# A fused two-model layer stack in emulated fp32: new work orders in its attention stages and feed-forward starts

## The chip, the cores and the metric

One NeuronCore of a Trainium2 chip runs the whole program, one launch, batch 1, 256 tokens, width 1024. The metric is device time in microseconds (us); smaller is better.

## The reference, cut to what matters

Two transformer models follow each other. The first has two layers: layer 0 mixes tokens with a gated delta rule beside an mLSTM, layer 1 with windowed attention (16 query heads in 4 groups, sinks). After each mixer come a squared-ReLU feed-forward and a gated addition. The second model has two layers with five attentions side by side (low-rank, forget-gated, block, differential, and one over a memory of 256 tokens) and a gated feed-forward with a short convolution. What the change touches:

```python
h = h + rmsnorm(ff, gains[3])                       # "post" factor, first model
gate = jax.nn.sigmoid(h @ w_ple_gate[layer])
h = h + gate * (p[layer] @ w_ple[layer])
...
q_e = _rms_norm(_heads(mem_q, N_HEADS_GROUP), mem_q_norm[l])
mem_kv = _rms_norm(mem, mem_norm[l]) @ mem_w_kv[l]
k_e, v_e = [_heads(t, N_HEADS_GROUP) for t in jnp.split(mem_kv, 2, axis=-1)]
o_e = _memory_attention(q_e, _rms_norm(k_e, mem_k_norm[l]), v_e, HEAD_DIM ** -0.5)
...
x = x + mixed @ w_o[l]
```

## The kernel before, in words

**Products.** Every large product is made of three fp32r matmuls (high by high, high by low, low by high; L495 to L497). Weights land in three raw slots by DMA from SyncE's queue. ScalarE casts a half of a panel to its high part (`scalar_split`, L684), VectorE subtracts to get the low part (`vector_split`, L786). There are four slots for such halves, so a cast waits until TensorE has used the half four before, and `split(upto)` runs up to three parts past `upto`. Activations are split in the same way (`hT`, `aT`, `memT`).

**Order.** There is no planner. Each engine has its own program, written out by hand, and semaphores tie them; an engine never overtakes a waiting instruction. The eight PSUM banks are filled in turn (`Banks.fill`): TensorE waits until the bank whose turn it is was read; banks that are still held for a long sum are passed over.

**Attention** (`tensor_attention`, `scalar_attention`, `vector_attention`). Groups of four heads go through a skewed pipeline. In step i TensorE does, in this order: the transposes of the output of group i-4 (`out_turned`), values of group i-3, transposes of the probabilities of i-2 (`turned`), scores of i-1, output products of i-4 (a panel of 48 matmuls into four held banks), and the transposes of queries and keys of group i (`prepared`). VectorE moves scores out of PSUM (L2180 to L2184), finds row maxima (L2190), and scales values (L2244). ScalarE does the exponentials (L2107), copies queries and keys (L2087/L2089), copies probabilities (L2124). Between these, generators (`between`, `amid`, `work`) put in other work: in the first model's layer 1 (mixer c, groups 0 to 3) the projection of the memory for both later layers (`mem_kv`, eight parts of 12 matmuls), in the second model's mixers (mixer 2, groups 0 to 5) the last columns of `w_in`. Group 5 of mixer 2 is the attention over the memory.

**Mixer 2, names.** Its queries are divided by their root mean square: squares on ScalarE, sums on VectorE, `means`, a square root on ScalarE (L716), a reciprocal on VectorE (L805), and a product (L2634). Outputs of finished groups are split into `m.out`, which is one slot of two chunks of `hT` here (`slots` = 1), four slots in mixer c.

**Starts of feed-forwards.** The sum of squares over features is taken by matmuls with ones: L667 over pairs 0 to 2, L670 over the last pair's squares, which ScalarE makes in `scalar_last_squares` (L741). After a feed-forward of the first model, L653/L658 do the same by token, then a root, a reciprocal, and L518 spreads the factor. `vector_turn_tables` builds the angles for sines and cosines, ScalarE applies Sin (L1720).

## Time and profile before

| | |
|---|---|
| median of 3 runs | 1517.23 us (1515.94 to 1520.54) |
| profiled execution, its own time | 1518.34 us |
| its span | 1517.0 us |
| mean granted TensorE clock | 0.979 |
| PE / DVE / ACT / POOL busy | 96% / 66% / 51% / 7% |
| moved by DMA | 228.19 MB, mean 150 GB/s |

PE is TensorE's matmul side, DVE VectorE, ACT ScalarE, POOL GpSimd. Positions in the text are us from the start of the span. A busy PE includes matmuls at half clock, so the granted clock has to be read beside it.

### The profile page before, as it was taken

What the parts mean: (1) busy time and instruction counts of PE and PEld (TensorE: products, weight loads), DVE (VectorE), ACT (ScalarE), POOL (GpSimd) and SP (SyncE); (2) the same over time, 40 slices, a digit from 0 to 9 for tenths busy, and PEclk for the clock granted to TensorE, in tenths of its full rate; (3) what the DMA queues carried; (4) which work ended last, traced back from release to release, by engine and by line L of the source; (5) the groups of instructions that cost most, each with busy time, mean ns of one, the idle gap of its engine ahead of it and who ended that gap; (6) DMA issues with size and microseconds to landing.
All of it is one profiled execution on the core that took longest, in us unless ns stands there. A gap on an engine that the chain in (4) does not pass through costs nothing.

```text
span 1517.0 us, 26059 instructions
## 1 busy us (share of the span) xinstructions
PE 1451.9 (96%) x10884; PEld 1376.7 (91%) x10884; DVE 997.7 (66%) x1503; ACT 777.5 (51%) x1219; POOL 110.4 (7%) x100
## 2 busy tenths in 40 slices
PE   7999989999998889999999989999999998999999
PEld 7989979999986789999997779999998787899999
DVE  5575676654678657654486765877755676577763
ACT  6744445444474544444376665544445685543443
POOL 0014112100001001110000000011100000011100
PEclk9999989999999999999999988999999998999999
DMA  8532245555463236655544312556555421255553
GB/s 260 161 111 84 61 155 179 191 182 182 158 202 132 73 107 190 184 182 194 180 155 153 120 59 72 176 170 190 175 193 189 137 84 56 90 181 177 190 177 105
DMA packets 186573, 228.19 MB, mean 150 GB/s; under 512 B 5964, under 2 KB 161228, under 8 KB 186456
## 3 DMA queue, kind: packets, MB, share of 16 engines
q1 hardware_dynamic: 185448, 221.75, 45.7%
q0 software_dynamic: 1008, 4.77, 0.9%
q8 instruction: 86, 1.41, 0.4%
q14 instruction: 31, 0.25, 0.1%
HBM read 225.46 MB, written 1.05 MB: 149 GB/s over the span
## 4 chain that ended last, share of the span: by engine, by line
PE 70%; DVE 17%; ACT 8%; issue 3%; DMA 1%; POOL 0%; DVEq 0%; ACTq 0%; SPq 0%; POOLq 0%
PE bank L495 20%; PE bank L497 20%; PE bank L496 20%; DVE weights_low L786 6%; ACT weights_high L684 3%; PE bank L503 2%; PE bank L1002 2%; ACT S L2107 2%; PE bank L2052 2%; DVE cv L2910 1%; PE bank L2031 1%; DVE S L2182 1%; DVE cv L2907 1%; DVE pad L2897 1%; DMA weights_raw<-in_w_in_ab 1%
## 5 line engine op out<-in xcount | busy, mean ns | idle before, releaser
L786 DVE TENSOR_TENSOR weights_low<-weights_raw,weights_high 128x1024 fp32r<-128x1024 f32 (+2 forms) x421 | 507.2, 1226 | 289.4 <-ACT weights_high L684 289.2
L684 ACT CAST weights_high<-weights_raw 128x1024 fp32r<-128x1024 f32 (+2 forms) x421 | 424.7, 1031 | 257.1 <-PE bank L497 254.8
L495 PE MATMUL bank<-hT_high,weights_high 128*128 128x256 f32 x1640 | 472.1, 288 | 15.3 <-DVE hT_low L858 5.0
L496 PE MATMUL bank<-hT_low,weights_high 128*128 128x256 f32 x1640 | 467.6, 285 | 0.0
L497 PE MATMUL bank<-hT_high,weights_low 128*128 128x256 f32 x1640 | 467.6, 285 | 0.0
L495 PEld LDWEIGHTS bank<-hT_high,weights_high 128*128 128x128 f32 x1640 | 318.1, 194 | 20.9 <-issue 9.8
L496 PEld LDWEIGHTS bank<-hT_low,weights_high 128*128 128x128 f32 x1640 | 318.0, 194 | 0.3
L497 PEld LDWEIGHTS bank<-hT_high,weights_low 128*128 128x128 f32 x1640 | 317.7, 194 | 0.2
L495 PE MATMUL bank<-aT_high,weights_high 128*128 128x256 f32 x864 | 242.3, 280 | 0.2
L496 PE MATMUL bank<-aT_low,weights_high 128*128 128x256 f32 x864 | 241.2, 279 | 0.0
L497 PE MATMUL bank<-aT_high,weights_low 128*128 128x256 f32 x864 | 241.1, 279 | 0.0
L495 PEld LDWEIGHTS bank<-aT_high,weights_high 128*128 128x128 f32 x864 | 162.2, 188 | 0.6 <-DVE weights_low L786 0.6
L497 PEld LDWEIGHTS bank<-aT_high,weights_low 128*128 128x128 f32 x864 | 162.3, 188 | 0.0
L496 PEld LDWEIGHTS bank<-aT_low,weights_high 128*128 128x128 f32 x864 | 161.7, 187 | 0.0
L495 PE MATMUL bank<-weights_high,hT_high 128*128 128x512 f32 (+1 forms) x288 | 115.0, 399 | 6.7 <-DVE weights_low L786 5.3
L497 PE MATMUL bank<-weights_high,hT_low 128*128 128x512 f32 (+1 forms) x288 | 111.2, 386 | 0.0
L496 PE MATMUL bank<-weights_low,hT_high 128*128 128x512 f32 (+1 forms) x288 | 111.2, 386 | 0.0
L2107 ACT ACTIVATE S<-S,mx 128x256 f32<-128x256 f32 (+1 forms) x128 | 57.2, 448 | 71.9 <-DVE mx L2190 49.7
L495 PEld LDWEIGHTS bank<-weights_high,hT_high 128*128 128x128 f32 x288 | 54.8, 190 | 19.5 <-DVE weights_low L786 6.1
L497 PEld LDWEIGHTS bank<-weights_high,hT_low 128*128 128x128 f32 x288 | 54.9, 191 | 10.4
L2862 ACT ACTIVATE cv<-cv 128x512 f32<-128x512 f32 x22 | 13.9, 633 | 95.9 <-DVE cv L2910 95.9
L496 PEld LDWEIGHTS bank<-weights_low,hT_high 128*128 128x128 f32 x288 | 55.0, 191 | 8.8
(417 smaller groups left out, 1830.8 us busy)
## 6 DMA issues: line engine op xcount, KB each, us to landing
weights_raw<-in_w_up SPq DMA_DIRECT2D x32, 1024.0 KB, 5.4
weights_raw<-in_w_down SPq DMA_DIRECT2D x32, 1024.0 KB, 5.1
weights_raw<-in_ffn_w_gate SPq DMA_DIRECT2D x22, 1024.0 KB, 5.3
weights_raw<-in_ffn_w_up SPq DMA_DIRECT2D x22, 1024.0 KB, 5.3
weights_raw<-in_w_in SPq DMA_DIRECT2D x20, 1024.0 KB, 5.0
weights_raw<-in_w_in_ab SPq DMA_DIRECT2D x16, 1024.0 KB, 5.9
weights_raw<-in_ffn_w_down SPq DMA_DIRECT2D x16, 1024.0 KB, 5.5
weights_raw<-in_w_o SPq DMA_DIRECT2D x10, 1024.0 KB, 6.1
```

The lines of the kernel that those rows point to most:

```text
L495: k.E.matmul(out, xh, wh, start=first, stop=False)
L496: k.E.matmul(out, xh, wl, start=False, stop=False)
L497: return k.E.matmul(out, xl, wh, start=False, stop=last)
L503: mm = k.E.transpose(bank[0:src.shape[-1], i * P:(i + 1) * P], src, k.ident)
L684: k.A.copy(w.halves(n)[0], w.raw_part(n)).then_inc(*k.s.weight_high(n))
L786: k.V.tensor_tensor(low, w.raw_part(n), high.bitcast(F32), ALU.subtract).then_inc(*k.s.weight_low(n))
L1002: mm = k.E.matmul(bank[:, hd * P:(hd + 1) * P], x(hd), y(hd), start=True, stop=True)
L2031: mm = E.matmul(bank[:, x * nk:(x + 1) * nk], m.QK[i][p0:p0 + d, c, t * P:(t + 1) * P], m.QK[i][p0:p0 + d, g.key_block(c), 0:nk], start=Tr ...
L2052: mm = E.matmul(bank[:, (t * 4 + hh) * 64:(t * 4 + hh + 1) * 64], m.PT[:, b, hh, :], g.values(hh, u), start=(x == 0), stop=(x == len(block ...
L2107: e = A.activation(m.S[:, i, hh, c0:c0 + nk], m.S[:, i, hh, c0:c0 + nk], ACT.Exp, bias=m.mx[:, i, t, hh:hh + 1], accum_out=m.den[:, i, t, ...
L2182: op = V.scalar_tensor_tensor(dst, bank, g.scale, spread(g.mask[:, c0:c0 + nk], 1, per), ALU.mult, ALU.add)
L2897: V.tensor_tensor(m.pad[:, q, :, 2:], k.banks[key][:, :].rearrange("p (k n) -> p k n", k=2), R, ALU.mult).then_inc(*k.banks.read(key))
```

## The change

Feed-forwards (both models): ScalarE makes the last pair's squares ahead of its first casts. The sine and cosine tables of layer 0 are built during the down projection. The sums by token after a feed-forward of the first model go into the next panel of 16 products: four products, the sums, three products, then the factor's transposes.

Mixer c: products are read out of their banks ahead of the last split of their panel; the keys are rotated before the memory is split; ScalarE alone copies queries and keys; two memory parts run at the first call instead of one; casts for the memory weights follow the steps 0, 0, 3, 3, 5, 5, 7; the memory's banks are read in `work(2)` and `work(4)` (ends of steps 1 and 3), and the second half of the query heads is rotated in `work(2)` instead of `work(1)`.

Mixer 2: two casts go ahead of the exponentials of group 0; one low half is made while a root is under way. The memory queries are no longer multiplied by their inverse root: their scores are, as they leave PSUM (sum plus 64 eps, so that the scale 1/8 is contained). The root for that is in `finish(3)` (step 6), no longer in `work(5)` (step 4). `m.out` has two slots.

All three attentions: the output of the last group is transposed amid the products of the group before it, after 9 of its 16.

```diff
@@ -811,14 +811,18 @@
     vector_inverse(k, st, r)
 
 
-def vector_token_linear(k, key, n0, evacuate=None, between=None):
+def vector_token_linear(k, key, n0, evacuate=None, between=None, evacuated_first=False):
     for k0 in (0, 4):
         n = k.w.first(key + (k0, n0))
         for i in range(2):
-            vector_split(k, n + i + 1)
-            if k0 + 2 * i == DC - 2 and evacuate is not None:
+            last = k0 + 2 * i == DC - 2 and evacuate is not None
+            if not (last and evacuated_first):
+                vector_split(k, n + i + 1)
+            if last:
                 for t in range(NT):
                     evacuate(t)
+            if last and evacuated_first:
+                vector_split(k, n + i + 1)
             if between is not None:
                 next(between, None)
 
...
@@ -1709,20 +1713,16 @@
     tensor_feature_major(k, ("p", layer), m.pt, 2)
     for p in range(4):
         tensor_pair_panels(k, st, p, m.aT, DFF1 // P, ("down", layer), lambda c: s.active.at((st, c - c % 2)))
-    tensor_sums_by_token(k, (st, "post"))
 
 
 def scalar_feed_forward_1(k, layer):
     A, s, m, st = k.A, k.s, k.ff1[layer], ("ff1", layer)
-    if layer == 0:
-        for which in range(2):
-            A.wait_ge(*s.angles.at(which))
-            A.activation(k.trig_table[:, which, :, :], k.trig_table[:, which, :, :], ACT.Sin).then_inc(*s.trig(which))
     for n0 in range(0, DFF1, 256):
         c, i = n0 // P, n0 // 256 % 2
+        if c == 0:
+            scalar_last_squares(k, st)
         scalar_split(k, k.w.first(("up", layer, 0, n0)) + 2)
         if c == 0:
-            scalar_last_squares(k, st)
             scalar_sums_root(k, st, m.R)
         A.wait_ge(*k.banks.was_read((st, c)))
         A.activation(m.aT[0][:, c:c + 2, :].rearrange("p k n -> p (k n)"), m.r[:, i, :], ACT.Square).then_inc(*s.relu_high((st, c)))
@@ -1731,6 +1731,10 @@
         for k0 in range(0, DFF1 // P, 8):
             scalar_split(k, k.w.first(("down", layer, k0, 256 * p)) + 2)
         scalar_out_squares(k, st, p)
+        if layer == 0 and p == 1:
+            for which in range(2):
+                A.wait_ge(*s.angles.at(which))
+                A.activation(k.trig_table[:, which, :, :], k.trig_table[:, which, :, :], ACT.Sin).then_inc(*s.trig(which))
     scalar_sums_root(k, (st, "post"), m.post_inv)
     for p in range(4):
...
@@ -1769,8 +1773,6 @@
 
 def vector_feed_forward_1(k, layer):
     V, s, m, st = k.V, k.s, k.ff1[layer], ("ff1", layer)
...
@@ -1793,6 +1795,8 @@
         for k0 in range(0, DFF1 // P, 8):
             vector_split(k, k.w.first(("down", layer, k0, 256 * p)) + 2)
         vector_out_gained(k, st, p, m.u, post_gain(k, layer, 1))
+        if layer == 0 and p == 0:
+            vector_turn_tables(k)
     vector_add_post(k, st, m, ("gate", layer), k.ple[layer].hT, None)
 
 
...
@@ -1820,8 +1824,11 @@
     held = tensor_hold(k, pst)
 
     def post_factor():
-        yield
-        yield
+        for _ in range(3):
+            yield
+        tensor_sums_by_token(k, (("ff1", layer), "post"))
+        for _ in range(3):
+            yield
         tensor_along_tokens(k, (("ff1", layer), "post"), k.ff1[layer].post_inv)
     tensor_deep_panel(k, pst, held, k.ff1[layer].pT, 0, ("ple", layer, 0, 0), k.banks.was_read((pst, "T", 0)), True, True, post_factor())
...
@@ -1919,33 +1926,41 @@
     vector_rms(k, "mem", m.inv)
 
 
+
+MEMORY_SPLITS = (0, 0, 3, 3, 5, 5, 7)
+
+
 def tensor_memory_projected(k):
 
-    for l in range(2):
-        yield from tensor_token_parts(k, ("mem", l), ("mem_kv", l), k.mem.memT[l], 0, 512)
+    parts = itertools.chain(*[tensor_token_parts(k, ("mem", l), ("mem_kv", l), k.mem.memT[l], 0, 512) for l in range(2)])
+    next(parts)
+    for _ in parts:
+        yield
 
 
 def scalar_memory_projected(k):
 
     n = k.w.first(("mem_kv", 0, 0, 0))
-    for part in range(8):
-        scalar_split(k, n + part - part % 2)
+    for upto in MEMORY_SPLITS:
+        scalar_split(k, n + upto)
         yield
 
 
 def vector_memory_projected(k):
 
-    n, m = k.w.first(("mem_kv", 0, 0, 0)), k.mem
-    for part in range(8):
-        vector_split(k, n + part - part % 2)
-        if part % 4 == 3:
-            l = part // 4
-            k.V.wait_ge(*k.s.inverse.at("mem"))
-            for t in range(NT):
-                key = (("mem", l), 0, t)
-                k.V.wait_ge(*k.s.products.at(key))
-                k.V.tensor_scalar(k.kvm[l][:, t, :], k.banks[key][:, :], m.inv[:, t:t + 1], None, ALU.mult).then_inc(*k.banks.read(key))
-        yield
+    n = k.w.first(("mem_kv", 0, 0, 0))
+    for upto in MEMORY_SPLITS:
+        vector_split(k, n + upto)
+        yield
+
+
+def vector_memory_evacuated(k, l):
+
+    k.V.wait_ge(*k.s.inverse.at("mem"))
+    for t in range(NT):
+        key = (("mem", l), 0, t)
+        k.V.wait_ge(*k.s.products.at(key))
+        k.V.tensor_scalar(k.kvm[l][:, t, :], k.banks[key][:, :], k.mem.inv[:, t:t + 1], None, ALU.mult).then_inc(*k.banks.read(key))
 
 
 def in_pairs(hh):
...
@@ -2054,6 +2075,10 @@
         mm.then_inc(*s.products((st, "values", n)))
 
     def out_turned(n):
+        if n < len(a.groups) - 1:
+            out_turned_now(n)
+
+    def out_turned_now(n):
         if a.groups[n].out is not None:
             E.wait_ge(*a.finished(k, n))
             tensor_feature_major(k, (st, "out T", n), a.groups[n].out[0], 2)
@@ -2066,7 +2091,14 @@
             held.extend(tensor_hold(k, st))
         _, j, k0 = g.out
         ready = k.banks.was_read(((st, "out T", n), "T", 0))
-        tensor_deep_panel(k, st, held, a.out, 2 * (j % a.slots), a.key + (k0, 0), ready, j == 0, n == len(a.groups) - 1)
+        amid = last_turned() if n == len(a.groups) - 2 else iter(())
+        tensor_deep_panel(k, st, held, a.out, a.out_chunk(n), a.key + (k0, 0), ready, j == 0, n == len(a.groups) - 1, amid)
+
+    def last_turned():
+
+        for _ in range(DC):
+            yield
+        out_turned_now(len(a.groups) - 1)
 
...
@@ -2079,7 +2111,7 @@
     before = a.slot_before(n)
     if before is not None:
         k.A.wait_ge(*k.s.products.at(a.last_scores(before)))
-    for c in range(0, g.blocks, 2 if a.copies_by_scalar else 4):
+    for c in range(0, g.blocks, 2):
         key, w = (st, "qk", n, c), min(2, g.blocks - c)
...
@@ -2180,6 +2198,8 @@
                     op = V.scalar_tensor_tensor(dst, bank, g.scale, g.bias[:, own, c0:c0 + nk], ALU.mult, ALU.subtract)
                 elif g.mask is not None:
                     op = V.scalar_tensor_tensor(dst, bank, g.scale, spread(g.mask[:, c0:c0 + nk], 1, per), ALU.mult, ALU.add)
+                elif g.query_factor is not None:
+                    op = V.tensor_tensor(dst, bank, spread(g.query_factor[:, t, own], 2, nk), ALU.mult)
                 else:
                     op = V.tensor_scalar(dst, bank, g.scale, None, ALU.mult)
...
@@ -2336,16 +2357,18 @@
             x = m.proj[:, t, c0:c0 + n * CHD].rearrange("p (n d) -> p n d", d=CHD)
             vector_rope(k, x, n, ROT_C, 0, t, m.tmp1, m.tmp2, ("c", c0, t))
     projected(1024)
+    turned_heads(1024, 4, 1024)
     vector_memory_turned(k)
     projected(0)
-    turned_heads(1024, 4, 1024)
     turned_heads(0, 8, 0)
     projected(512)
     V.tensor_scalar(m.minus_sink, k.row(1, "sinks"), -1.0, None, ALU.mult).then_inc(*s.minus_sink("c"))
     V.wait_ge(*s.minus_sink.at("c"))
 
     def work(n):
-        if n == 1:
+        if n in (2, 4):
+            vector_memory_evacuated(k, n // 2 - 1)
+        if n == 2:
             turned_heads(512, 8, 512)
 
...
@@ -2405,9 +2428,10 @@
         Group(4, P, in_fours(0), 32 ** -0.5, True, values(C_DIFF + 512), None, mask=cneg, gains=heads_2(k, l, "diff")),
         Group(4, P, in_fours(1), 32 ** -0.5, True, values(C_DIFF + 512), out(2), mask=cneg, shared=True),
         Group(4, P, in_pairs, 64 ** -0.5, True, values(C_MOBA + 512), out(3), mask=cneg, gains=heads_2(k, l, "moba")),
-        Group(4, P, in_pairs, 64 ** -0.5, False, lambda hh, u: kvm[:, u, 256 + hh * 64:256 + (hh + 1) * 64], out(4), gains=heads_2(k, l, "mem")),
+        Group(4, P, in_pairs, 64 ** -0.5, False, lambda hh, u: kvm[:, u, 256 + hh * 64:256 + (hh + 1) * 64], out(4), gains=heads_2(k, l, "mem"),
+              query_factor=m.st[:, :, SLOT["memq"]:SLOT["memq"] + 4]),
     ]
-    return Attention(("m2", l), m, groups, 1, ("o_2", l), m.out, copies_by_scalar=True, late=(1,))
+    return Attention(("m2", l), m, groups, 2, ("o_2", l), m.out, copies_by_scalar=True, late=(1,))
 
 
 def projected_to(k, l, end):
...
@@ -2485,7 +2509,6 @@
             for mark in projected_to(k, l, D_IN2):
                 E.wait_ge(*mark)
         else:
-            E.wait_ge(*s.normed.at((l, "memq")))
             for mark in projected_to(k, l, D_IN2):
                 E.wait_ge(*mark)
...
@@ -2563,8 +2586,8 @@
         n2, n5 = [k.w.first(("in_2", l, 0, n0)) for n0 in (2048, 2560)]
         squared_columns("moba", C_MOBA, 512)
         scalar_root(k, (st, "mla"), m.st2[:, :, 0:20])
-        yield
-        scalar_split(k, n2 + 1)
+        scalar_split(k, n2 + 2)
+        yield
         for t in range(NT):
             evacuated(2048, t)
         squared_columns("diff", C_DIFF, 512)
@@ -2583,14 +2606,11 @@
             scalar_split(k, k.w.first(("in_2", l, 0, 2560)) + 4)
             squared_columns("memq", C_MEM, 256)
 
-    def work(n):
-        if n == 5:
-            roots("memq", SLOT["memq"], 4)
-
     def finish(n):
         if n == 3:
+            roots("memq", SLOT["memq"], 4)
             scalar_root(k, (st, "sub"), m.st2[:, :, 0:4])
-    scalar_attention(k, k.attention_2[l], work, finish, last_columns(), amid)
+    scalar_attention(k, k.attention_2[l], None, finish, last_columns(), amid)
     for p in range(4):
         scalar_residual(k, ("ff2", l), p, st, k.hT, ff2_gain(k, l))
 
...
@@ -2648,9 +2671,13 @@
         V.wait_ge(*s.products.at((st, n0, t)))
         V.tensor_scalar(m.hp[:, t, n0:n0 + nn], k.banks[st, n0, t][:, 0:nn], m.inv[:, t:t + 1], None, ALU.mult).then_inc(*k.banks.read((st, n0, t)))
 
-    def scaled(*kinds):
+    def scaled(*kinds, meanwhile=lambda: None):
         first, end = SLOT[kinds[0][3]], SLOT[kinds[-1][3]] + kinds[-1][1]
-        inverses(kinds[0][3], m.st[:, :, first:end], spread(k.const("inv_d")[:, first:end], 1, NT))
+        name, x = kinds[0][3], m.st[:, :, first:end]
+        means(name, x, spread(k.const("inv_d")[:, first:end], 1, NT))
+        meanwhile()
+        vector_inverse(k, (st, name), x)
+        V.wait_ge(*s.inverse.at((st, name)))
         for c0, n, d, name in kinds:
             normed(name, m.hp[:, :, c0:c0 + n * d], n, m.st[:, :, SLOT[name]:SLOT[name] + n],
...
@@ -2722,7 +2749,7 @@
         vector_split(k, n2 + 1)
         yield
         squared(DIFF)
-        scaled(DIFF)
+        scaled(DIFF, meanwhile=lambda: vector_split(k, n2 + 2))
         turned_heads("diff", C_DIFF, 16, 32, ROT_D, ROT_C + ROT_A + ROT_M)
...
@@ -2777,10 +2804,13 @@
             vector_split(k, k.w.first(("in_2", l, 0, 2560)) + 4)
 
     def work(n):
+
         if n == 5:
             squared(MEMQ)
-            scaled(MEMQ)
+            V.wait_ge(*s.reduced.last())
+            V.tensor_scalar(queries, queries, 64 * EPS, None, ALU.add).then_inc(*s.mean((st, "memq")))
     a = k.attention_2[l]
...
@@ -2798,7 +2828,10 @@
             then(V.scalar_tensor_tensor(m.d1, m.d2, m.lm[:, 66:67], m.d1, ALU.mult, ALU.add))
             then(V.tensor_tensor(m.d2, m.d1, m.d1, ALU.mult))
             V.tensor_reduce(m.st2[:, :, 0:4], m.d2.rearrange("p t (n d) -> p t n d", n=4), AXX, ALU.add).then_inc(*s.reduced((l, "sub")))
-            inverses("sub", m.st2[:, :, 0:4], 1.0 / 64)
+            means("sub", m.st2[:, :, 0:4], 1.0 / 64)
+            vector_inverse(k, (st, "memq"), queries)
+            vector_inverse(k, (st, "sub"), m.st2[:, :, 0:4])
+            V.wait_ge(*s.inverse.at((st, "sub")))
             for t in range(NT):
...
@@ -2854,9 +2887,10 @@
     A, s, m, st = k.A, k.s, k.ff2[l], ("ff2", l)
     for n0 in range(0, DFF2, 256):
         c, i = n0 // P, n0 // 256 % 3
+        if c == 0:
+            scalar_last_squares(k, st)
         scalar_split(k, k.w.first(("ff_gate", l, 0, n0)) + 2)
         if c == 0:
-            scalar_last_squares(k, st)
             scalar_sums_root(k, st, m.R)
         A.wait_ge(*s.conv.at((st, c, 1)))
         A.activation(m.cv[:, i, :, :], m.cv[:, i, :, :], ACT.Silu).then_inc(*s.silu((st, c)))
```

## Rows read from the trace of the kernel before

**Rows 1.** The page: the span.
```profile
span 1517.0 us, 26059 instructions
```
**Rows 2.** Waits of PE over the span: what waited for what, total us, times, longest.
```profile
PE bank L495 <- DVE weights_low L786: 7.6, 4, 2.7
...
PE bank L670 <- ACT pair_squares L741: 4.9, 3, 3.2
...
PE bank L495 <- DVE hT_low L796: 4.3, 3, 1.5
```
**Rows 3.** Windows: stretch, length, busy (x) PE PEld DVE ACT POOL, PEclk, DMA, GB/s.
```profile
224.31:228.60 4.29, 4.29 (x21) 4.20 (x20) 2.44 (x2) 1.14 (x3) 0.62 (x1) 0.50 0.79 244
...
893.29:949.34 56.05, 49.74 (x355) 46.04 (x353) 29.72 (x49) 33.12 (x79) 0.00 (x0) 0.85 0.23 75
1256.39:1312.48 56.09, 47.88 (x354) 43.95 (x353) 29.73 (x49) 32.82 (x79) 0.00 (x0) 0.88 0.22 74
...
587.00:754.00 167.00, 166.63 (x1404) 166.66 (x1404) 93.79 (x95) 72.00 (x79) 19.30 (x17) 1.00 0.59 189
```
**Rows 4.** Timeline, feed-forward start of layer 0: start, length, engine, line, [idle before <-releaser].
```profile
218.55 0.38 PE L667 MATMUL bank<-pair_sum,consts 128*128 128x256 f32 x1
...
222.80 0.80 PE L670 MATMUL bank<-pair_squares,consts 128*128 128x256 f32 x1 [3.22 <-ACT pair_squares L741]
...
224.31 0.78 PE L495 MATMUL bank<-hT_high,weights_high 128*128 128x256 f32 x1
```
**Rows 5.** Timeline of PE, feed-forward start of layer 1.
```profile
579.33 0.38 PE L667 MATMUL bank<-pair_sum,consts 128*128 128x256 f32 x1
...
587.37 0.35 PE L495 MATMUL bank<-hT_high,weights_high 128*128 128x256 f32 x1 [0.41 <-DVE weights_low L786]
```
**Rows 6.** Timeline of PE, behind the feed-forward of layer 0.
```profile
399.76 0.38 PE L658 MATMUL bank<-consts,pair_squares 128*128 128x1 f32 x2 [0.90 <-ACT pair_squares L741]
...
401.82 0.27 PE L518 MATMUL bank<-consts,post_inv 128*128 128x128 f32 x1
...
410.24 0.35 PE L495 MATMUL bank<-gate_hT_high,weights_high 128*128 128x256 f32 x1 [0.41 <-DVE gate_hT_low L856]
```
**Rows 7.** Timeline of PE in the first mixer 2.
```profile
865.39 0.43 PE L495 MATMUL bank<-weights_high,hT_high 128*128 128x356 f32 x1 [2.68 <-DVE weights_low L786]
...
898.80 0.30 PE L503 MATMUL bank<-consts,S 128*128 128x128 f32 x1 [1.42 <-ACT QK L2089]
...
902.37 0.47 PE L503 MATMUL bank<-consts,S 128*128 128x128 f32 x1 [2.43 <-DVE hT_low L796]
```
**Rows 8.** Timeline of ACT in the first mixer 2.
```profile
899.25 1.28 ACT L716 ACT_TABLE_LOAD   x1
900.54 0.21 ACT L716 ACTIVATE st<-st 128x8 f32<-128x8 f32 x1
900.66 0.57 ACT L695 CAST hT_high<-bank 128x512 fp32r<-128x512 f32 x1
...
925.11 0.51 ACT L2107 ACTIVATE S<-S,mx 128x256 f32<-128x256 f32 x1 [4.31 <-DVE mx L2190]
```
**Rows 9.** Timeline of DVE in the first mixer 2.
```profile
901.63 0.68 DVE L796 TENSOR_TENSOR hT_low<-bank,hT_high 128x512 fp32r<-128x512 f32 x1
...
907.66 0.69 DVE L2182 SCALAR_TENSOR_TENSOR S<-bank,consts 128x512 f32<-128x512 f32 x1 [0.15 <-PE bank L2031]
...
921.46 2.48 DVE L2184 TENSOR_SCALAR S<-bank 128x512 f32<-128x512 f32 x4 [0.20 <-DVE mixed L2806]
```
**Rows 10.** Timeline of DVE in mixer c.
```profile
474.94 0.41 DVE L946 TENSOR_TENSOR tmp<-proj,trig 128x256 f32<-128x256 f32 x1
...
479.19 1.28 DVE L2182 SCALAR_TENSOR_TENSOR S<-bank,consts 128x512 f32<-128x512 f32 x2
...
494.06 1.41 DVE L1947 TENSOR_SCALAR kvm<-bank,mem_inv 128x512 f32<-128x512 f32 x2
```
**Rows 11.** Timeline of PE in mixer c.
```profile
494.87 0.48 PE L503 MATMUL bank<-consts,k 128*128 128x128 f32 x1 [2.04 <-DVE kvm L1947]
```

39 lines of the change are left out of this document (16 added, 23 removed).

## The prediction

> **What bounds the kernel now.** I read the page first, then the waits of TensorE (PE), then windows for its clock, then the timeline around each idle stretch. The profiled execution took 1518.34 us, its span is 1517.0 us [rows 1], so 1.34 us lie around the span. The median of the runs shown is 1517.23, 1.1 below the profiled one. PE is busy for 96% of the span, so a gain is idle PE time or half-clock time that comes back. Two kinds of stretch must be told apart. In the first model's second up-and-down projection 1404 matmuls take 167 us at clock 1.00, 0.119 us each, with no idle time [rows 3]: there PE is the bound, and a microsecond won at the start stays won. In the attention stages matmuls are short, and the work goes round PE, VectorE (DVE) and ScalarE (ACT).
>
> The second kind is seen in the two mixers 2. From the query transposes of group 4 to the last output panel the first takes 56.05 us at a mean clock of 0.85, the second 56.09 us at 0.88 [rows 3]. The engine that had the better clock gained nothing. So a chain through DVE and ACT bounds most of this stretch, and PE's idle time there is the result of it.
>
> **Feed-forward starts.** In layer 0, PE has summed three pairs at 218.55 and waits 3.22 us for the last squares, since ACT first does two sine tables and two casts; L670 starts at 222.80, the next features at 224.31 [rows 4]. The wait is followed by a stretch at 0.50, in which 21 matmuls take 4.29 us [rows 3]. A panel has 48; the other 27 take 27 x 0.119 = 3.2. So from L667 to the next panel: 5.76 + 4.29 + 3.2 = 13.25 us. The change takes both causes away, and layer 1, which has no tables there, is the pattern: 587.37 - 579.33 = 8.04, with a wait of 0.41 for a low half included [rows 5]. Gain **5.2**. Bounds: 3.2, the wait alone; 6.0, if the 0.41 goes too.
>
> In the two gated feed-forwards the squares wait behind casts only. PE's waits for L741 are 4.9 us in three, the longest 3.2 [rows 2], so the two others have 1.7. ACT now waits for a pair sum ahead of its casts, but PE still has four ready halves. Gain **1.7** (bounds 0 and 1.7; in layer 1 of the first model there is no such wait, so nothing).
>
> The tables move into the down projection. DVE needs some 3 us for them, while a half there lasts 24 x 0.119 = 2.9 us of PE and four are ready, so they are hidden; if that cover is gone, they cost up to 3. ACT must load the square root's table again, 1.28 us [rows 8], beside PE's products.
>
> **Sums amid products (two places).** Now L658 starts at 399.76 after a wait of 0.90, and L518 at 401.82, 2.06 later with three products between [rows 6]. In the new order PE does four products (12 matmuls, 1.4 us) ahead of the sums and nothing waits: L653 starts at 397.9 + 1.4 = 399.3, L658 0.9 later at 400.2, L518 at about 402.25. The idle 0.90 is filled, but the factor comes 0.4 us later, and what ends last behind it is DVE's chain to the next activations: PE waits for them at 410.24 anyway [rows 6]. So this edit *costs* 0.4 each, **-0.9** together (bounds: -1.5, and +0.9 each if that second wait were not there).
>
> **Last output turned amid products (three places).** PE's waits in L495 for L796 are 4.3 us in three, longest 1.5 [rows 2]. These are the waits in front of the last output panel. The transposes now come after 9 of 16 products, some 2.5 us before that panel begins, and need ACT 0.57 and DVE 0.68 [rows 8, 9]. All 4.3 go, 1.43 per stage. The second slot of `m.out` makes that possible and takes no wait away by itself.
>
> **Mixer 2 (two of them, alike).** First, PE's 2.68 us for a low half at 865.39 [rows 7] go, as cast and low half are made ahead. But the casts stand in front of the exponentials of group 0: the second waits for PE's second part, and the exp table (1.28) is loaded behind it, so these start nearly 1 us later. And behind the wait the next thing that ends late is group 1's exponentials and the copies behind them. Of 2.68 I take half, 1.3 (bounds 0 and 2.7).
>
> Second, in step 4 ACT does table load and root for the memory queries (899.25 to 900.66) before it copies group 1's output [rows 8]: 1.4 off the queue. DVE then has no product L2634 in front of its low part (901.63 [rows 9]), 0.4 more. So PE's third transposed block moves from 902.37 [rows 7] by 1.3 + 1.4 + 0.4 = 3.1. Its wait of 2.43 becomes some 0.6.
>
> Third, the clock. From 902.37 to the last scores that DVE takes at 907.66 [rows 9] are 5.3 us for 4 transposes and 16 score matmuls, at half clock; at full clock it would be 2.9. If the clock holds, the scores are 3.1 + 2.4 = 5.5 earlier, and with them the exponentials of group 4, the casts, the copies of group 5 and DVE's work on the differential output. The root now sits there beside one that already needed the square root's table, so it adds no load; it adds one reciprocal (0.2). Scores of group 5 leave PSUM by a product of two operands instead of one with a constant: L2182, with two tensors, has 0.68 to 0.69 for 512 elements, L2184 2.48 for four [rows 9], so nothing. Exponentials of group 5 (925.11 [rows 8]) start 5.3 earlier, and PE, whose panel of 48 needs 5.8 us, is not late for them.
>
> With the last panel: 5.3 + 1.4 = 6.7. If the clock does not hold: 4.3; with a second half-clock stretch under the late panel: 2.8. Which? New idle time of 1.4 and 0.6 us stands close together in short matmuls; before it was 1.42 and 2.43. That lies between what lost the clock and what did not, so I take **5.4** for each mixer, last panel included.
>
> The Trainium skill (TensorE: Matmul & The Clock Gate, Terms) prices time at half clock at half of it. By that rule the mixers at 0.85 and 0.88 would lose 8.4 and 6.7 us to the clock, and the second should be 1.7 us shorter; rows 3 have them equal, so the trace disagrees for this stage. In the dense stretch of layer 0 it agrees (21 matmuls, 4.29 instead of 2.5 us). It gives the first rival below its most.
>
> The skill (ScalarE: Activation LUTs, What ACT_TABLE_LOAD costs) counts 1.28 us and a drain of 1.38 for each change of table set. In rows 8 the root starts 0.01 us after the load: no drain. By the rule the exponentials of group 0 would start 1.4 us later still, and the sum would be up to 2.8 us smaller.
>
> **Mixer c.** DVE before: rotation of the second query heads from 474.94, the first scores taken only at 479.19 [rows 10]. With the rotation moved, and one memory part more before the scores, I count scores 3.4 us earlier and one part (2.75 us) ahead. But then the memory's banks: their reads wait for `work(2)`, behind three low halves. By the order of `Banks.fill` the transposed probabilities of group 0 now fall on those two banks (before, they were passed over as held), and the values of group 1 on the next two. I put these waits at 4.3 and 4.7 us; before one such wait took 2.04 [rows 11], and a pair of reads takes 1.41 [rows 10]. The rotation (4.25 us) now stands in front of the scores of group 1. By step 4 the lead is used up: first output panel at 525 to 527, before at 524. So -0.5 there and +1.4 for the last panel: **+0.9** (bounds: -12 and +6).
>
> **Sum.** 5.2 + 1.7 - 0.9 + 2 x 5.4 + 0.9 = 17.7. On the profiled execution 1518.34 - 17.7 = 1500.6; 1.1 lower for the median: **1499.5 us**.
>
> **Rivals.**
> A. The clock holds and mixer c keeps its lead. Mixers 2 give 6.7 each, mixer c 4.3 + 1.4: 5.2 + 1.7 - 0.9 + 13.4 + 5.7 = 25.1, so 1492. For: each wait has its cause named. Against: the bank order. The rule on half-clock time would add all of mixer 2's low-clock time, another 15 us: 1477. I give that 3 in 100.
> B. The wait moves. In both mixers the clock stays low and the panel is slowed (2.8 each), mixer c loses 6: 5.2 + 1.7 - 0.9 + 5.6 - 4.6 = 7.0, 1510.
> C. Slower: the memory's banks in mixer c. If none of their delay overlaps: bank waits 4.3 + 4.7, rotation 4.0, low halves in front of group 2's scores 1.9, half-clock stretches behind both waits 3.4 each, together 21.7, and mixers 2 as in B: 5.2 + 1.7 - 0.9 + 5.6 + 1.4 - 21.7 = -8.7, 1526. It decides from about 13 us of loss in mixer c. Against: the DVE delays lie inside the bank waits.
> D. No change: mixers 2 give nothing but the last panel (2.9) and mixer c loses 7: 1515.
>
> **Chances.** Forecast 0.50 (own range 1495 to 1505), A 0.22, B 0.17, D 0.06, C 0.05. The range that leaves 2 in 10 out: 1488 to 1511. About 0.3% (4.6 us) is what a measurement of this kernel tells from no change. Faster 0.89, same 0.06, slower 0.05.
>
> **What would show it.** After: L670 right behind L667 in layer 0, no half-clock stretch there, 8 us to the next panel. Waits for L741 gone. L518 2.0 to 2.1 us after L658, and longer waits for `gate_hT_low`. No wait of L495 for L796. In mixer 2 no wait for a low half before group 2's transposes, ACT's copy of group 1's output right behind the copies of QK, exponentials of group 5 some 5 us earlier relative to the first scores. In mixer c waits of PE for L1947 of 4 us and more. The forecast is wrong if the mixers 2 shrink by less than 4 or more than 8 us each, or if mixer c changes by more than 4.

## The result

The changed kernel takes 1506.4 us (median of 4 runs, 1502.47 to 1508.67), the kernel before, timed beside it, 1517.92 (4 runs, 1515.94 to 1520.54). The ratio is 0.9921, 95% interval 0.9903 to 0.9940. By the ratio that is 12.0 us faster (9.1 to 14.7); the medians are 11.5 apart. The prediction said 1499.5, so a gain of 17.7 where 12.0 came. The time lies inside its outer range of 1488 to 1511 and the direction is right, but it lies outside the forecast's own range of 1495 to 1505, and a third of the gain is missing. The profiled executions are 10.45 us apart (1518.34 and 1507.89; of the kernel before [rows 1]).

```profile
span 1506.6 us, 26045 instructions
```

To see where the time went, I cut both executions at the same work: the places at which PE adds up the sums of squares, L653 (sums by token) and L667 (sums of a feed-forward). Lengths in us:

| stretch | before | after | gain | foretold |
|---|---|---|---|---|
| start to the first sums (same code) | 198.53 | 199.99 | -1.5 | 0 |
| layer 0's feed-forward sums to mixer c | 219.75 | 214.64 | 5.1 | 4.8 |
| mixer c | 121.18 | 123.71 | **-2.5** | 0.9 |
| layer 1's feed-forward sums to mixer 2 | 214.27 | 214.64 | -0.4 | -0.4 |
| mixer 2, first and second | 168.47, 168.44 | 164.45, 164.47 | **4.0**, 4.0 | 5.4 each |
| gated feed-forward, first | 194.71 | 194.16 | 0.5 | 0.9 |
| gated feed-forward, last, to the end | 191.82 | 190.11 | 1.7 | 0.9 |

(Two stretches of 20 us in front of the first feed-forwards are left out; they lose 0.2 and 0.35, and vary by up to 1.0 with the same code.) In all executions below the first row lies between 197.4 and 201.7 with the same code. That may be most of what separates two runs of one kernel; as each kernel has one profiled execution, it is not shown. The rows from layer 0's sums to mixer c and from layer 1's to mixer 2 stay within 0.05 us of each other unless their own code is touched, so there the stretches tell more than the whole time does. The attention stages don't repeat like that. Mixer c, with the changed kernel's code, took 121.7 to 124.9 us in six executions. Mixer 2, with that code, took 162.3 to 164.8 in fourteen instances (seven executions). Of the kernel before there is one execution, so the -2.5 and the 4.0 are known to 2 or 3 us only.

The waits of PE after, answering [rows 2]: what waited for what, total us, times, longest.

```profile
PE bank L503 <- ACT S L2139: 8.8, 6, 2.0
...
PE bank L503 <- DVE kvm L1963: 4.7, 1, 4.7
PE bank L495 <- DVE weights_low L786: 4.2, 4, 2.0
PE bank L2073 <- DVE kvm L1963: 3.7, 1, 3.7
PE bank L503 <- ACT QK L2121: 3.1, 2, 1.8
PE bank L495 <- DVE gate_hT_low L860: 3.0, 4, 1.0
```

In the kernel before, the waits for `kvm` and for exponentials were:

```profile
PE bank L503 <- ACT S L2107: 3.2, 5, 1.7
...
PE bank L503 <- DVE kvm L1947: 2.0, 1, 2.0
PE bank L495 <- DVE kvm L1947: 2.0, 1, 2.0
```

Gone are L670 for L741 and L495 for L796, as foretold. The waits for `kvm` (the memory's projected keys and values, which VectorE reads out of their banks) in mixer c grew from 4.0 to 8.4 us. The first row, PE waiting for exponentials, grew from 3.2 to 8.8, all of it in the mixers 2.

Layer 0's feed-forward start, answering [rows 4]; timeline of PE.

```profile
220.18 1.02 PE L667 MATMUL bank<-pair_sum,consts 128*128 128x256 f32 x4
221.04 1.03 PE L670 MATMUL bank<-pair_squares,consts 128*128 128x256 f32 x4
...
228.22 0.36 PE L495 MATMUL bank<-hT_high,weights_high 128*128 128x256 f32 x1 [0.41 <-DVE weights_low L786]
```

L670 stands right behind L667, and the next panel begins 8.04 us behind L667, to the hundredth what layer 1 showed before [rows 5]. Behind the feed-forward of layer 0, answering [rows 6]:

```profile
396.30 1.03 PE L658 MATMUL bank<-consts,pair_squares 128*128 128x1 f32 x8
...
398.35 0.60 PE L518 MATMUL bank<-consts,post_inv 128*128 128x128 f32 x4
...
406.76 0.36 PE L495 MATMUL bank<-gate_hT_high,weights_high 128*128 128x256 f32 x1 [0.95 <-DVE gate_hT_low L860]
```

L518 comes 2.05 us behind L658, and the wait for the low half is 0.95 where it was 0.41.

The first mixer 2, PE, answering [rows 7]:

```profile
872.52 2.79 PE L503 MATMUL bank<-consts,S 128*128 128x128 f32 x12 [2.04 <-ACT S L2139]
...
902.26 2.31 PE L2052 MATMUL bank<-QK 64*128 64x128 f32 x16 [0.20 <-DVE gb L2264]
```

and ACT, answering [rows 8]:

```profile
848.71 0.79 ACT L684 CAST weights_high<-weights_raw 128x712 fp32r<-128x712 f32 x1 [3.51 <-PE bank L497]
849.52 1.28 ACT L2139 ACT_TABLE_LOAD   x1
850.81 0.40 ACT L2139 ACTIVATE S<-S,mx 128x128 f32<-128x128 f32 x1
...
898.80 1.23 ACT L2121 ACTIVATE QK<-bank,cols 128x512 f32<-128x512 f32 x2
899.93 0.56 ACT L695 CAST hT_high<-bank 128x512 fp32r<-128x512 f32 x1
...
922.49 0.51 ACT L2139 ACTIVATE S<-S,mx 128x256 f32<-128x256 f32 x1 [4.30 <-DVE mx L2210]
```

The wait of 2.68 for a low half is gone, and one of 2.04 for exponentials stands in its place, which was not there. Twelve transposes behind it take 2.79 us: half clock. The copy of group 1's output follows right behind the QK copies, without root and table load, as foretold. Two windows of the changed kernel, the half-clock stretch behind that wait and the whole mixer (columns as in [rows 3]):

```profile
871.40:885.10 13.70, 12.52 (x51) 11.03 (x51) 8.11 (x12) 9.79 (x29) 0.00 (x0) 0.50 0.00 0
...
793.37:957.82 164.45, 156.74 (x989) 137.75 (x989) 111.33 (x214) 106.86 (x221) 0.69 (x2) 0.94 0.33 108
```

In mixer c, PE answering [rows 11] and DVE answering [rows 10]:

```profile
484.82 1.97 PE L503 MATMUL bank<-consts,S 128*128 128x128 f32 x8 [4.72 <-DVE kvm L1963]
...
514.94 1.30 PE L2073 MATMUL bank<-proj,PT 128*128 128x64 f32 x10 [3.69 <-DVE kvm L1963]
...
521.44 4.21 PE L2052 MATMUL bank<-QK 64*128 64x128 f32 x16
525.58 0.58 PE L495 MATMUL bank<-hT_high,weights_high 128*128 128x256 f32 x1
```

```profile
472.46 1.89 DVE L2200 SCALAR_TENSOR_TENSOR S<-bank,consts 128x512 f32<-128x512 f32 x3 [4.17 <-PE bank L2052]
...
480.61 3.50 DVE L786 TENSOR_TENSOR weights_low<-weights_raw,weights_high 128x1024 fp32r<-128x1024 f32 x3 [3.93 <-ACT weights_high L684]
484.02 1.40 DVE L1963 TENSOR_SCALAR kvm<-bank,mem_inv 128x512 f32<-128x512 f32 x2
```

The products for `kvm` ended at 479.67; DVE reads their banks at 484.02, behind three low halves. The first of these waited 3.93 for its cast, and the other two followed at once. PE waits for that bank. Behind each of the two waits lie some 10 us at half clock; the 16 score matmuls (4.21 us there) take 2.34 at full clock.

### The profile page after: what moved, and what is told of

The parts are those of the page before. It is cut to its first block, busy times and chain, and to the rows that moved or that the text cites. A ratio compares the mean times of both kernels' runs of the same rounds, so it can differ in the third digit from the quotient of the medians.

```text
span 1506.6 us, 26045 instructions
## 1 busy us (share of the span) xinstructions
PE 1452.7 (96%) x10884; PEld 1378.7 (92%) x10884; DVE 994.2 (66%) x1495; ACT 774.3 (51%) x1219; POOL 108.8 (7%) x100
## 3 DMA queue, kind: packets, MB, share of 16 engines
q8 instruction: 86, 1.41, 0.4%
## 4 chain that ended last, share of the span: by engine, by line
PE 71%; DVE 18%; ACT 7%; issue 3%; POOL 0%; DMA 0%; ACTq 0%; DVEq 0%; SPq 0%; POOLq 0%
PE bank L495 20%; PE bank L497 19%; PE bank L496 19%; DVE weights_low L786 7%; ACT weights_high L684 3%; PE bank L503 3%; PE bank L1006 2%; PE bank L2052 2%; PE bank L2073 2%; DVE cv L2944 2%; ACT S L2139 2%; DVE cv L2941 1%; DVE S L2200 1%; DVE pad L2931 1%; DVE cv L2950 1%
## 5 line engine op out<-in xcount | busy, mean ns | idle before, releaser
L495 PE MATMUL bank<-hT_high,weights_high 128*128 128x256 f32 x1640 | 471.5, 288 | 10.4 <-DVE hT_low L862 4.8
L495 PEld LDWEIGHTS bank<-hT_high,weights_high 128*128 128x128 f32 x1640 | 316.6, 193 | 16.5 <-issue 9.4
L495 PE MATMUL bank<-aT_high,weights_high 128*128 128x256 f32 x864 | 241.9, 280 | 0.2
L495 PEld LDWEIGHTS bank<-aT_high,weights_high 128*128 128x128 f32 x864 | 162.3, 188 | 0.6 <-DVE weights_low L786 0.6
L495 PE MATMUL bank<-weights_high,hT_high 128*128 128x512 f32 (+1 forms) x288 | 115.7, 402 | 1.4 <-DVE weights_low L786 1.4
L2139 ACT ACTIVATE S<-S,mx 128x256 f32<-128x256 f32 (+1 forms) x128 | 57.2, 449 | 62.4 <-DVE mx L2210 40.5
L495 PEld LDWEIGHTS bank<-weights_high,hT_high 128*128 128x128 f32 x288 | 55.2, 192 | 14.2 <-issue 5.4
```

The source lines that it names most:

```text
L495: k.E.matmul(out, xh, wh, start=first, stop=False)
L2139: e = A.activation(m.S[:, i, hh, c0:c0 + nk], m.S[:, i, hh, c0:c0 + nk], ACT.Exp, bias=m.mx[:, i, t, hh:hh + 1], accum_out=m.den[:, i, t, ...
```

## The experiments

Times are medians, each with its ratio to the kernel before on the same chip; stretches come from the profiled execution. "Group n at x" is the time from the stage's first sums to the start of group n's exponentials on ACT, with groups counted from 0 as in the kernel. The edits are shortened; `...` and lines in words stand for what is left out. Each stretch is from one execution, so differences in the attention stages have to be held against the spreads given above.

**Mixer c's edits undone.**
```
-        vector_token_linear(..., evacuate, side, evacuated_first=True)
+        vector_token_linear(..., evacuate, side)
-MEMORY_SPLITS, vector_memory_evacuated in work(2), work(4)
+the three *_memory_projected of before, turned_heads(512, 8, 512) at n == 1
+turned_heads(1024, 4, 1024) behind projected(0) again
+QK copies of block 2 by VectorE (vector_heads_turned)
```


> The changed kernel with every edit of mixer c undone (the order of its leads, the order in which the memory's weights are split and its banks read, the copies of QK shared by ScalarE and VectorE); all else stays changed. The stage (from its first sums by token to the next ones) took 121.2 us in the kernel before and 123.7 in the changed one. Theory 1, the edits of mixer c cost what the prediction took for a gain of 0.9: the stage comes back to 121.2 +- 0.5, the kernel gains about 2.5 on the changed one (1506.4), to 1504, and keeps the lead of 4.4 us of the scores of the first group no longer. Theory 2, the 2.5 us are spread between two executions and the edits are neutral: the stage stays near 123.7 or falls anywhere between, in no relation to the waits for kvm, and the time stays at 1506.

Measured: 1502.47 us, ratio 0.9898 (0.9875 to 0.9921); mixer c 118.6. Theory 2 falls. But theory 1 had the size wrong: the stage falls 2.6 below that of before. Of this, 1.4 is the wait in front of the last output panel, whose edit is kept. The other 1.2 is the clock and no edit: before, 12 memory matmuls behind the first wait for `kvm` ran at half clock and took 4.3 us; here they take 3.1, and the half-clock stretch lies earlier, in front of a wait. So mixer c's own edits cost some 4 to 5 us here, not 2.5.

**The memory's banks read one place earlier.**
```
     for i, upto in enumerate(MEMORY_SPLITS):
+        if i in (2, 6):
+            vector_memory_evacuated(k, i // 4)
         vector_split(k, n + upto)
...
-        if n in (2, 4):
-            vector_memory_evacuated(k, n // 2 - 1)
```


> The changed kernel, with the memory's banks read by VectorE one place earlier, ahead of the next pieces of weight_low and not behind them (both layers' memories). Theory 1, the two waits of TensorE for kvm (4.7 and 3.7 us) and the clock that is lost behind each (10.2 us at 0.5) make mixer c long: the waits shrink to under 1.5 us each, the clock holds in one of the two places at least, and the stage falls from 123.7 to 117 to 120; the kernel to 1500 to 1503. Theory 2, TensorE is not what bounds the stage there (VectorE and ScalarE carry the chain of a group): the waits shrink all the same, others grow in their place, and the stage stays within 1 us of 123.7.

Measured: 1497.05 us, ratio 0.9855 (0.9831 to 0.9879); mixer c 113.9, 9.8 less than in the changed kernel, more than theory 1 asked. PE's waits in the stage:

```profile
PE bank L503 <- DVE proj L955: 2.0, 1, 2.0
PE bank L495 <- DVE weights_low L786: 1.4, 1, 1.4
PE bank L2054 <- DVE mixed L2266: 1.1, 1, 1.1
```

None is for `kvm`, and only 6.9 us of the stage are at half clock, where 20.4 were. VectorE pays nothing for it: the two reads fall into the time in which it had waited for a cast, and the first of the three low halves starts at 45.8 of the stage in both kernels.

**And the last query heads turned a group earlier.**
```
     def work(n):
-        if n == 2:
+        if n == 1:
             turned_heads(512, 8, 512)
```


> The kernel c_banks_early (the memory's banks read one place earlier; 1497.05 us, mixer c 113.9) with the turn of the last eight query heads one group earlier again, as in the kernel before: 4.9 us of VectorE that stand behind the low halves and ahead of the second group's scores there (exps of group 1 at 56.8 us of the stage) go into the 4.2 us in which VectorE waits for the first group's scores. Theory 1, VectorE's order sets the pace of mixer c from the first group on: the exps of group 0 come 0.7 to 1.5 us later, those of group 1 3.5 to 4.5 earlier, the stage falls to 109.5 to 112, the kernel to 1493 to 1495.5. Theory 2, once the banks are free TensorE's own work and clock bound the stage: the exps of group 1 come earlier and the stage stays within 1 us of 113.9.

Measured: 1493.87 us, ratio 0.9838 (0.9817 to 0.9859); mixer c 108.3, below theory 1's span. So the place of this rotation, which the change had also moved, costs another 5.6 us once the banks come free in time. DVE:

```profile
468.37 0.43 DVE L950 TENSOR_TENSOR tmp<-proj,trig 128x256 f32<-128x256 f32 x1
...
472.64 1.88 DVE L2202 SCALAR_TENSOR_TENSOR S<-bank,consts 128x512 f32<-128x512 f32 x3
...
480.79 3.50 DVE L786 TENSOR_TENSOR weights_low<-weights_raw,weights_high 128x1024 fp32r<-128x1024 f32 x3 [0.28 <-ACT weights_high L684]
...
484.80 1.88 DVE L2202 SCALAR_TENSOR_TENSOR S<-bank,consts 128x512 f32<-128x512 f32 x3
```

The turn fills the 4.2 us in which DVE had waited for the first scores. Group 0 starts at 40.5 (40.4 without the edit), group 1 at 52.7 (56.8). The whole stage now runs at full clock:

```profile
434.84:543.17 108.33, 104.70 (x678) 91.44 (x677) 84.48 (x151) 63.22 (x146) 4.85 (x10) 1.00 0.40 133
```

**The memory's part alone undone.**
```
-MEMORY_SPLITS, vector_memory_evacuated in work(2), work(4)
+the three *_memory_projected of before, turned_heads(512, 8, 512) at n == 1
 (evacuated_first and ScalarE's copies stay)
```


> The changed kernel with only the memory's part of mixer c undone (order of its splits and products, place at which its banks are read, turn of the last eight query heads at group 1); the new order of the leads and ScalarE's copies stay. The stage takes 123.7 so, and 118.6 with all of mixer c's edits undone. Theory 1, the memory's order costs more than 5.1 us and the leads give some 3: the exps of group 0 stay at 40.4 us of the stage, it falls to 113.5 to 117, the kernel to 1498 to 1501. Theory 2, the leads give nothing in the end, since the next groups wait for the same things: 118 to 119.5, the kernel at 1502. Theory 3, the leads and copies cost too: above 120.

Measured: 1499.17 us, ratio 0.9869 (0.9854 to 0.9884); mixer c 115.7, group 0 at 40.5. Theory 1. Against the 118.6 above, the new leads and copies give 2.9 us; the memory's part costs 8.0 (123.7 against 115.7). This part is three edits in one: the order, the place of the reads and the place of the rotation. With the reads early and the rotation where it was before, the new order is 7.3 us *better* than the old (108.3 against 115.7).

**Mixer 2: the early cast undone.**
```
-        scalar_split(k, n2 + 2)
         yield
+        scalar_split(k, n2 + 1)
-        scaled(DIFF, meanwhile=lambda: vector_split(k, n2 + 2))
+        scaled(DIFF)
```


> The changed kernel with the early cast and the early low half of mixer 2 undone in both mixers. Theory 1, the early cast gave the first groups nothing in the end, since a new wait of 2.04 us for the exps of group 1 and 13.7 us of half clock stand in its place: undone, the wait of 2.7 us of TensorE for the low half comes back, the wait of 2.04 us goes, and each mixer 2 stays within 0.7 us of 164.5; the kernel at 1505 to 1508. Theory 2, it gives its part and the loss is elsewhere: each mixer 2 becomes longer by 1.3 to 2.7 us and the kernel goes to 1509 to 1512.

Measured: 1509.35 us, ratio 0.9942 (0.9920 to 0.9963); mixers 164.8 and 164.9, against 164.45. The wait of 2.7 is back, that of 2.04 gone, and 0.4 us is the difference: theory 1 by the stages. The whole time lies in theory 2's span, but mixer c was 1.2 longer with the same code, and the interval overlaps that of the changed kernel. The 0.4 is made of two parts: group 2 starts at 86.4, as before the change, and so 1.0 earlier than the changed kernel's 87.4, but then the clock falls between groups 3 and 4, which takes 12.5 and not 11.1.

**Mixer 2: the new wait filled.**
```
     def turned(n):
+        if st[0] == "m2" and n == 1:
+            (bank b: the one that the transposes below will fill; waits until it is read)
+            for _ in range(10):
+                E.matmul(k.banks.psum[b], k.hT[0][:, 0, 0:P], k.hT[0][:, 0:2, :], ...)
         for t in range(NT):
             E.wait_ge(*s.exps.at((st, n, t)))
```


> The changed kernel with ten more matmuls of 512 columns in each mixer 2, ahead of the wait for the exps of group 1, into the bank that the transposes behind them overwrite: some 2.1 us of work in place of the wait of 2.04. They compute nothing that is used. Theory 1, the clock that falls behind that wait is what ate the gain: with the wait filled the stretch of 13.7 us at 0.5 is gone or under 4 us, the second half of the groups comes 1.3 to 3 us earlier and each mixer 2 falls from 164.5 to 161.5 to 163.2; the kernel to 1501 to 1504. Theory 2, the chain of a group runs over VectorE and ScalarE and TensorE's clock has slack there: the stretch is gone, and each mixer 2 stays within 0.5 of 164.5. Theory 3, the clock falls all the same, and nothing changes but a wait filled.

Measured: 1507.61 us, ratio 0.9926 (0.9905 to 0.9947), so no difference in the whole time, outside theory 1's 1501 to 1504; the mixers 162.45 and 163.9. PE in the first:

```profile
871.50 2.56 PE L2066 MATMUL bank<-hT_high 128*128 128x512 f32 x10
873.90 1.47 PE L503 MATMUL bank<-consts,S 128*128 128x128 f32 x12
```

The window that answers to the half-clock stretch, at the same place of the stage:

```profile
872.61:886.31 13.70, 12.83 (x97) 11.24 (x97) 9.63 (x15) 11.88 (x34) 0.00 (x0) 1.00 0.13 42
```

This mixer starts at 794.58, the changed kernel's at 793.37. So the transposes start 0.2 us later in the stage than there (79.3 and 79.15) and end 1.15 earlier, at 1.47 us in place of 2.79. The 13.7 us that were at half clock are at full clock, and group 2 starts at 85.3 and not 87.4. In the second mixer group 2 is as early, but the clock falls at 105.3 us of the stage, and 1.4 us are lost there. Theory 1 in the first, half of it in the second.

The same gain also comes without the fill when the clock happens to hold. In the first mixer 2 of "mixer c's edits undone", whose mixer code is the changed kernel's, PE:

```profile
868.75 1.50 PE L503 MATMUL bank<-consts,S 128*128 128x128 f32 x12 [2.04 <-ACT S L2144]
```

The wait is the same 2.04, the twelve transposes take 1.50, group 2 starts at 85.3 and the mixer takes 162.3. Over all runs, without the fill (and with the early cast) the clock held like this in 2 of 18 instances, once group 2 started at 86.3, and in the other 15 at 86.8 to 87.5. With the fill it started at 85.3 or 85.4 in all six. So the fill does not add a gain of its own; it makes sure of the one that the early cast should have given.

**Both waits for exponentials filled, with the memory's banks read early.**
```
-        if st[0] == "m2" and n == 1:            for _ in range(10):
+        if st[0] == "m2" and n in {1: 10, 4: 8}:    for _ in range({1: 10, 4: 8}[n]):
```


> The kernel c_banks_early (1497.05 us; its mixers 2 take 164.0 and 163.8) with matmuls that compute nothing used in each mixer 2: ten ahead of the wait for the exps of group 1, eight ahead of that for group 4. Theory 1, the clock decides between two courses: with the first wait filled (alone that gave 162.5 in one mixer and 163.9 in the other, where the clock fell 1.4 us of idle later) and the later one too, both mixers come to 161.5 to 162.8, the kernel to 1494 to 1496. Theory 2, the clock falls in the idle time between the two and the late group loses what the early one won: the mixers stay at 163.5 to 164.5, the kernel at 1496 to 1498.

Measured: 1496.32 us, ratio 0.9856 (0.9833 to 0.9880); mixers 162.4 and 162.4. Theory 1 in the mixers. The whole time lies in theory 2's span, and its ratio is that of the kernel without the fills (0.9855), so no gain is shown there.

**The inverse root of the memory queries put back.**
```
+            E.wait_ge(*s.normed.at((l, "memq")))
+    def work(n): if n == 5: roots("memq", SLOT["memq"], 4)
-            V.tensor_scalar(queries, queries, 64 * EPS, None, ALU.add)
+            scaled(MEMQ)
-        query_factor=m.st[:, :, SLOT["memq"]:SLOT["memq"] + 4]
... (and the root and its inverse no longer in finish(3))
```


> The changed kernel with the inverse root of the memory queries computed and multiplied into the queries ahead of their transposes again. Between the exps of group 4 and of group 5 of mixers 2 lay 14.5 us before, and 11.1 (clock held between them) or 12.6 (clock fallen) in the changed kernel and its relatives. Theory 1, the prediction's (1.8 us in its second piece): back to 14.2 to 14.6, each mixer 2 longer by 1.6 to 3.4, the kernel at 1510 to 1513. Theory 2, the gain between these groups comes from the low half that no longer stands in front of group 2's transposes (the two output slots): under 1 us each, 1506.5 to 1508.5.

Measured: 1513.49 us, ratio 0.9966 (0.9951 to 0.9981); mixers 167.6 and 167.4, 14.4 us between the two groups (the expectation counts them from one: they are groups 3 and 4). Theory 1, near its upper end: between these groups the edit is worth 3.3 us, over the stage 3.1 and 3.0, the largest part of mixer 2. ACT and PE:

```profile
898.83 1.28 ACT L716 ACT_TABLE_LOAD   x1
900.12 0.21 ACT L716 ACTIVATE st<-st 128x8 f32<-128x8 f32 x1
900.24 0.57 ACT L695 CAST hT_high<-bank 128x512 fp32r<-128x512 f32 x1
```

```profile
901.95 0.67 PE L503 MATMUL bank<-consts,S 128*128 128x128 f32 x4 [2.43 <-DVE hT_low L796]
```

The wait of 2.43 is the same as in [rows 7].

**The last output rows turned as before.**
```
-        if n < len(a.groups) - 1:
-            out_turned_now(n)
+        out_turned_now(n)
...
-        amid = last_turned() if n == len(a.groups) - 2 else iter(())
+        amid = iter(())
```


> The changed kernel with the last output rows of every attention turned ahead of the last but one panel again, and not amid its products. Theory 1, the prediction's 1.43 us each: the time from the last group's exps to the end of the stage, 35.3 us in mixers 2 now and 37.0 before, returns to 36.7 to 37.0, mixer c grows by 1.2 to 1.6 (to 125), the kernel to 1509.5 to 1511.5. Theory 2, the low halves of the last rows are awaited somewhere else anyway: under 0.5 us each, 1506 to 1507.5.

Measured: 1511.82 us, ratio 0.9954 (0.9939 to 0.9970). From the last exponentials to the end of mixers 2 it takes 36.96 us again, where it was 35.33: 1.63 each. Mixer c grew by 4.8, more than either theory gave, since the clock fell there for 17 us in one stretch, where it was 10. The whole time is 0.3 above theory 1's span. Theory 1, but in mixer c its size is mixed with the clock. The waits in front of the last panels are back as they were in [rows 2]:

```profile
PE bank L495 <- DVE hT_low L796: 4.3, 3, 1.5
```

**Sines and turned tables back at the start.**
```
     if layer == 0:
+        for which in range(2): A.wait_ge(*s.angles.at(which)); A.activation(..., ACT.Sin)
+        vector_turn_tables(k)
```


> The changed kernel with the sines and the turned tables back at the start of layer 0's first feed-forward (the casts stay ahead of the squares' remainder, as changed). From its sums to the sums of mixer c the kernel before took 219.75 us and the changed one 214.64, in each of its relatives too. Theory 1, the prediction's: ScalarE's two sines with their table loads and VectorE's turned tables stood ahead of the first factor, and they make nearly all of the 5.2 us: back there, the stretch returns to 219.2 to 219.9, the kernel to 1510.5 to 1512.5. Theory 2, the casts ahead of the squares are what counts: the stretch stays below 217.

Measured: 1509.97 us, ratio 0.9945 (0.9926 to 0.9963); the stretch takes 218.22. It lies between the two theories: of the 5.1 us the tables are 3.6. The other 1.5 hold three things that no run separates: the squares ahead of the casts, the half-clock stretch of 4.29 us of [rows 3] (here the clock is 1.00 throughout), and the 0.4 that the moved sums cost. In this edit the squares stay ahead of the casts, as in the changed kernel; the expectation has that the wrong way round.

```profile
219.98 1.13 PE L670 MATMUL bank<-pair_squares,consts 128*128 128x256 f32 x4 [1.33 <-ACT pair_squares L741]
```

**The sums by token back at the feed-forward's end.**
```
+    tensor_sums_by_token(k, (st, "post"))        (end of tensor_feed_forward_1)
-        tensor_sums_by_token(k, (("ff1", layer), "post"))   (amid the panel)
```


> The changed kernel with the sums by token of both first feed-forwards back at their end, where the kernel before has them, and not amid the products that follow. From the sums of layer 1's feed-forward to mixer 2 the kernel before took 214.27 us, the changed one and its relatives 214.64 to 214.67. Theory 1, the prediction's: the move costs 0.4 us each time, so the stretch returns to 214.2 to 214.3 and the one of layer 0 falls from 214.64 to 214.2, the kernel gains 0.8: 1505.5, too little for the whole time to show. Theory 2, the loss comes from another edit: both stretches stay at 214.65.

Measured: 1507.02 us, ratio 0.9925 (0.9907 to 0.9944). Layer 1: 214.39, 0.26 less, theory 1 with a smaller size. Layer 0: 215.6, 0.9 *more*. There the wait of 0.90 came back, and this time the clock fell behind it:

```profile
396.83:400.25 3.42, 3.42 (x17) 3.42 (x17) 0.88 (x3) 0.53 (x2) 0.00 (x0) 0.50 0.72 229
```

17 matmuls in 3.42 us and not 17 x 0.119 = 2.0: 1.4 lost, without which it would be 214.2, as theory 1 has it. The same wait stood in the kernel before [rows 6] with no fall behind it.

**All finds together:** banks early, heads turned at group 1, both waits filled.

> Both finds together: the memory's banks read earlier and the last query heads turned at group 1 (mixer c 108.3 us, kernel 1493.9), and the two waits of mixer 2 filled (ten and eight matmuls, mixers 162.4 each and not 164.2). Theory 1, the parts add: mixer c 108.3, mixers 2 162.4 each, the kernel 3.6 us below 1493.9, at 1490.3 (1489 to 1492). Theory 2, the clock falls elsewhere in the mixers 2 as the starts shift: 163.5 to 164.5, 1493 to 1494.

Measured: 1490.66 us, ratio 0.9816 (0.9801 to 0.9831), the fastest here: by the ratio 27.9 us below before (27.5 between the medians), 15.7 below the changed kernel. Mixer c 108.3, mixers 2 162.5 and 164.8: theory 1 in the whole time and the first mixer, theory 2 in the second. Of the 27.9, 12.9 are mixer c.

## Why the prediction was right, and where it was wrong

**Feed-forward starts: right.** Layer 0 was foretold at 5.2, or 4.8 with the moved sums, and its stretch gave 5.1. Of this 3.6 are the tables; the rest is not taken apart. In the first gated feed-forward 0.5 came of the 0.86, and its wait is gone; the last gives 1.7, but it varies by as much with one code (189.7 to 191.3).

**Sums amid products: right in layer 1** (0.3 to 0.4 against 0.4), and in layer 0 only once the 1.4 us of the clock are taken off. The filled wait also takes away a place at which the clock can fall.

**Last output panel: right.** 1.43 foretold, 1.63 measured in mixers 2.

**Mixer 2: mechanism right, size wrong.** Of 5.4 each, 4.0 came (4.02 and 3.97, so on the very edge of the prediction's own sign of being wrong, less than 4). By terms, from the starts of groups (before and after, first mixer): group 2 at 86.4 and 87.4, from group 3 to 4 14.5 and 11.1, from group 5 to the end 36.96 and 35.33. Group 5 itself starts 2.4 earlier in the stage, where 5.3 was foretold. So

- "Of 2.68 I take half, 1.3" is the step that failed: group 2 came 1.0 *later*. The early cast moved group 1 by only 0.3 (75.8 to 75.4). The idle time went over to the wait for these exponentials, 2.04 us, and the clock fell behind it for 13.7 us, over just the transposes and scores on which groups 2 and 3 hang. Filled, or in the two instances in which the clock held by itself, group 2 starts at 85.3, 1.1 earlier than before: the foretold 1.3 was there, and the clock took it and more.
- The 5.4 left 2.7 for the second piece and the clock (5.4 - 1.3 - 1.4). 3.4 came, since the clock held between groups 3 and 4; in relatives in which it fell there (12.6 us between them) it is 1.9. The mechanism is the one foretold: with the root put back the 3 us go.
- Together -1.0 + 3.4 + 1.6 = 4.0.
- Before, [rows 3] had two mixers of one length at clocks of 0.85 and 0.88, and I took from it that the clock is of little weight there. What counts is under which work it falls: 13.7 us at 0.5 in front of group 2 cost 2.1 us (87.4 against 85.3).

The Trainium skill (TensorE: Matmul & The Clock Gate, Terms) prices time at half clock at half of it, which as an estimate would be 6.9 us for those 13.7. The runs give 2.1, so it doesn't hold in this stage; in a dense stretch it nearly does (1.4 of 3.42, above). The Trainium skill (ScalarE: Activation LUTs, What ACT_TABLE_LOAD costs) also counts a drain of 1.38 us with each load of a table. The trace after has no room for it on either side: the load starts 0.02 behind the end of the cast before it (849.50), and the exponentials start at 850.81, 0.01 behind the load's end.

**Mixer c: wrong, by 3.4 us** (1.5 to 4.6 over the six executions of this code, always in the direction of a loss). Each piece was close: the lead of the first group 3.4 foretold, 3.25 measured; bank waits 4.3 and 4.7, measured 4.72 and 3.69 (but the kernel before already had two of 2.0, and the prediction names one). What failed is the step "By step 4 the lead is used up: first output panel 525 to 527, before at 524". Counted from the stage's start, that panel begins at 90.8 and not at 85.9: 4.9 later, not 1 to 3, since I left the half clock behind both waits to the slower rival alone. It took 10 us twice, and both times the next scores lay in it, 1.9 us longer each. Of that 4.9 the last panel gave back 1.4, and the first panel another 1.0, since before it ran longer at half clock (7.3 us against 6.3); this leaves 2.5. The experiments name the cause: the place at which the banks are read costs 9.8. The place of the rotation costs another 5.6 with the banks early: it takes group 1 from 52.7 to 56.8, and the prediction priced it only as a delay that the lead would cover. The leads give 2.9, and the new order itself, with both of these put right, 7.3.

**Rivals.** The result lies between the forecast and B: the wait did move in the mixers 2 (B gave them 2.8 each), and mixer c lost 2.5 where B had it lose 4.6. C named what made mixer c long, half clock behind both bank waits, but gave the stage a loss of 20.3, eight times the measured one. Both large terms missed on the same side, so the total was not helped by luck; it lies in the outer range because that range was wide.
